# Eight landing places for the first conditioning panels, and the linear attention's decays made among the even features

## The reference, cut to what matters

```python
cond = jax.nn.silu(c)
mod = (cond @ w_ada[l] + b_ada[l]).reshape(B, N_SUB, 3, D_MODEL)
y = swiglu(modulate(x, mod, 0), ffn_w_in[l, 0], ffn_w_out[l, 0])
...
log_a = [(jax.nn.log_sigmoid(((h @ a1[d]) @ a2[d] + ab[d]).astype(jnp.float32)) / GLA_TAU)
         .reshape(bsz, t, GLA_HEADS, GLA_DK) for d in range(2)]
qk = jax.nn.silu(dwconv1d(jnp.concatenate([mq, mk], axis=-1), conv_w, conv_b))
```

## Time and profile before

| what | value |
|---|---|
| median of the runs | 3091.85 us |
| the profiled execution's own time | 3098.78 us |
| its span, first to last instruction | 3096.8 us |
| TensorE matmuls busy | 2802.9 us (91%) |
| VectorE | 1875.1 us (61%) |
| ScalarE | 1033.0 us (33%) |
| GpSimd | 197.4 us (6%) |
| mean granted clock of TensorE | 0.952 |
| moved by DMA | 469.59 MB, mean 152 GB/s |

### The profile page before, as it was taken

The page is one execution under the profiler, slowest core; times in us unless marked ns, Lnnn a source line. Parts: engine busy times, 40 slices in busy tenths (PEclk is TensorE's granted clock), DMA queues, the critical chain, the costliest instruction groups (busy, mean ns, idle before and its releaser), DMA issues.

```text
span 3096.8 us, 47653 instructions
## 1 busy us (share of the span) xinstructions
PE 2802.9 (91%) x18018; PEld 2359.1 (76%) x18018; DVE 1875.1 (61%) x3213; ACT 1033.0 (33%) x1331; POOL 197.4 (6%) x89
## 2 busy tenths in 40 slices
PE   2999999999999998999899556999999899979998
PEld 2998877899998887899778444587744767748887
DVE  5785354677775854667474466477732676662881
ACT  1432132443532124153443552333300644431211
POOL 0000000000000000000044000144300000000000
PEclk9999999999999998999999678999999999969999
DMA  7786633577574842456242100222234221103441
GB/s 260 275 315 253 230 108 123 204 272 285 206 270 163 321 141 96 163 177 234 93 178 95 63 1 34 82 95 90 103 158 160 83 81 55 68 14 123 150 174 70
DMA packets 109673, 469.59 MB, mean 152 GB/s; under 512 B 7020, under 2 KB 60856, under 8 KB 62136
## 3 DMA queue, kind: packets, MB, share of 16 engines
q1 hardware_dynamic: 109496, 467.19, 41.7%
HBM read 466.10 MB, written 1.06 MB: 151 GB/s over the span
## 4 chain that ended last, share of the span: by engine, by line
issue 53%; PE 31%; DVE 7%; DVEq 4%; ACT 2%; POOLq 1%; ACTq 1%
PE accs L786 9%; PE accs L674 4%; PE accs L687 2%; PE accs L689 2%; PE accs L688 2%; DVEq L2574 2%; PE accs L1134 2%; PE accs L1135 1%; PE accs L1136 1%; DVE arena L2551 1%; DVE normed L86 1%; POOLq L1339 1%; PE mix L1185 1%; ACT arena L76 1%; PE mix L833 1%
## 5 line engine op out<-in xcount | busy, mean ns | idle before, releaser
L687 PE MATMUL accs<-normed_r,arena_r 128*128 128x256 f32 (+2 forms) x1864 | 585.6, 314 | 20.4 <-DVE cond_panel_r L86 6.1
L688 PE MATMUL accs<-arena_r 128*128 128x256 f32 (+1 forms) x2090 | 594.8, 285 | 0.0
L689 PE MATMUL accs<-normed_r,panel_r 128*128 128x256 f32 (+2 forms) x1872 | 585.5, 313 | 0.0
L674 PE MATMUL accs<-normed,panel 128*128 128x256 f32 x2176 | 485.3, 384 | 6.3 <-ACTq L469 3.0
L674 PEld LDWEIGHTS accs<-normed,panel 128*128 128x128 f32 x2176 | 415.2, 192 | 71.1 <-ACTq L469 4.3
L86 DVE TENSOR_TENSOR panel_r<-panel,arena_r 128x1024 fp32r<-128x1024 f32 (+1 forms) x240 | 319.8, 1332 | 129.8 <-ACTq L1378 90.7
L688 PEld LDWEIGHTS accs<-arena_r 128*128 128x128 f32 x2090 | 395.4, 189 | 2.2 <-issue 0.2
L687 PEld LDWEIGHTS accs<-normed_r,arena_r 128*128 128x128 f32 (+1 forms) x1864 | 351.1, 188 | 56.4 <-issue 12.9
L1377 ACT ACTIVATE arena_r<-panel 128x1024 fp32r<-128x1024 f32 (+1 forms) x240 | 275.4, 1147 | 303.7 <-PE accs L689 115.3
L689 PEld LDWEIGHTS accs<-normed_r,panel_r 128*128 128x128 f32 (+1 forms) x1872 | 350.9, 187 | 23.9
L2551 DVE SCALAR_TENSOR_TENSOR arena<-accs,vectors,arena 128x189 f32<-128x189 f32 (+2 forms) x704 | 279.5, 428 | 94.6 <-issue 63.4
(11 more groups left out here) (375 smaller groups left out, 4175.5 us busy)
## 6 DMA issues: line engine op xcount, KB each, us to landing
panel<-w SPq DMA_DIRECT2D x250, 1024.0 KB, 4.9
panel<-w SPq DMA_DIRECT2D x48, 1408.0 KB, 7.9
cond_panel<-wc SPq DMA_DIRECT2D x56, 1024.0 KB, 6.9
normed<-wc SPq DMA_DIRECT2D x48, 1024.0 KB, 7.6
arena<-wc SPq DMA_DIRECT2D x16, 1024.0 KB, 6.0
residual<-xs SPq DMA_DIRECT2D x2, 1024.0 KB, 8.3
residual<-crows SPq DMA_DIRECT2D x2, 512.0 KB, 9.3
arena<-cond_row_kept SPq DMA_DIRECT2D x2, 512.0 KB, 6.7
```

Source lines behind the costliest of these rows:

```text
L674: mm = pe.matmul(acc[b][:, o:o + ntok], w[:, k * PANEL + j * P:k * PANEL + j * P + P], rhs(k), start=(k == 0), stop=(k == KD - 1))
L687: pe.matmul(out, hi[:, k, 0:m], src_hi(k), start=clear and k == 0, stop=False, skip_group_check=True)
L688: pe.matmul(out, hi[:, k, 0:m], src_lo(k), start=False, stop=False, skip_group_check=True)
L689: mm = pe.matmul(out, lo[:, k, 0:m], src_hi(k), start=False, stop=last and k == n - 1, skip_group_check=True)
```

## The change

Two things, which share no stage.

In the head every one of the eight conditioning panels gets a landing place of its own: the two of before, the first half of the residual tile, and five regions of the arena that hold nothing yet. SP issues all eight with no wait; the vectors come after panel 1, the latents after panel 4, weight panel 0 after panel 5, weight panel 1 after panel 7, then constants, tables and weight panels 2 and 3. No semaphore is new: panels 2 and 3 share one, 4 and 5 share one, and later waits on these are raised. VectorE weighs panels 0 and 1 before its arithmetic, 2 to 4 in the middle of it, 5 to 7 after it, and makes the low part of weight panel 0 after panel 6. The barrier of the head is gone. The first input is made two chunks at a time with a signal for each pair, and the low part of weight panel 1 between the third pair and the last. The bias matmul and its copy go behind weight panel 3 of `in00`.

In the even stage TensorE does the four decay matmuls after feature panel 0. ScalarE adds the bias into the unused ends of the four weight slots and takes the magnitude during panel 1, Exp before panel 2 and Ln before panel 3; VectorE combines them before the convolutions. Silu of the convolved channels goes from panels 12 and 13 to the beginnings of panels 10 and 11. After the barrier VectorE copies the combined decays into `logd` and clears `gsuff`, for one direction and then the other, and only then clears `gpairs` and masks the near product.

The diff, in the order of the program: tiles, semaphores, then SyncE, TensorE, ScalarE and VectorE.

```diff
+        head_slots = [H[:, :, 0:T], cond_slot1[:, :, :], X[:, :, 0:T]] + [region(2048 * i, KD, PANEL) for i in range(HEAD - 3)]
...
-        gabs = region(E_T + 2048, 2, 1024)
+        decay_kept = [t[:, KD * PANEL:KD * PANEL + 512] for t in slots]
+        decay_ln = [region(E_T + 8192, 2, 512), region(13312, 2, 512)]
...
+        head_landed = [(cond_landed[0], 16), (cond_landed[1], 16), (S("context_loaded"), 32), (S("context_loaded"), 32),
+                       (S("masks_loaded"), 32), (S("masks_loaded"), 32), (S("pair_loaded"), 16), (S("hankel"), 16)]
...
-            load_cond("head", 0, 0)
-            load_cond("head", 0, 1)
-            sp.dma_start(cols[:, :], io["cols"]).then_inc(S("cols_loaded"), 16)
+            for i in range(HEAD):
+                sp.dma_start(head_slots[i], wc[i:i + 1, :, :].rearrange("a p (k c) -> p (a k) c", k=KD)).then_inc(head_landed[i][0], 16)
+                if i == 1:
+                    sp.dma_start(cols[:, :], io["cols"]).then_inc(S("cols_loaded"), 16)
+                if i == 4:
+                    sp.dma_start(X[:, :, lat], xs[:, :, lat]).then_inc(S("latents_moved"), 16)
+                if i == 5:
+                    load_static(G["in00"], 0)
+            load_static(G["in00"], 1)
             sp.dma_start(cst[:, m1:NCST], io["consts"][:, m1:NCST]).then_inc(S("consts_loaded"), 16)
+            sp.dma_start(cst[:, 0:m0], io["consts"][:, 0:m0]).then_inc(S("loaded"), 16)
             sp.dma_start(poolw[:, :, :, :], io["poolw"]).then_inc(S("loaded"), 16)
             sp.dma_start(relb[:, :], io["rel_bias"]).then_inc(S("loaded"), 16)
+            load_static(G["in00"], 2)
+            load_static(G["in00"], 3)
             sp.wait_ge(S("consts_loaded"), 16)
             sp.dma_start(a2w[32:96, :], io["a2w"]).then_inc(S("loaded"), 16)
-            for i in range(2, HEAD):
-                load_cond("head", 0, i)
...
-            def gla():
+            def decays():
+
                 pe.wait_ge(S("rank_ready"), 1)
...
-                pe.wait_ge(S("decay_read"), 2)
...
-            pe.wait_ge(S("loaded"), 80)
-            pe.matmul(mix[0:4, 0, 0:384], relb[:, :], const("onehot")[0:32, :], start=True, stop=True).then_inc(S("bias_mm"), 1)
-            stage_end(pe, count)
...
                         split_up(G[name], it, u, 2 * l + f)
+                        if name == "in00" and isinstance(it, int) and (it, u) == (0, 3):
+                            pe.wait_ge(S("loaded"), 64)
+                            pe.matmul(mix[0:4, 0, 0:384], relb[:, :], const("onehot")[0:32, :], start=True, stop=True).then_inc(S("bias_mm"), 1)
...
                             kept_features(G["even"], 0, u, 0)
+                        if u == 0:
+                            decays()
+                    pe.wait_ge(S("decay_read"), 2)
...
-                for d in range(2):
-                    act.wait_ge(S("decay_mm"), d + 1)
...
+                            if step == 0:
+                                act.wait_ge(S("decay_mm"), d + 1)
+                                for c in range(2):
+                                    act.eng.activation(decay_kept[2 * d + c], mix[:, 2 * d + c, :], ACT.Identity, bias=col("gla_ab_2", 2 * d + c))
+                                act.drain().then_inc(S("decay_read"), 1)
+                            elif step == 1:
+                                for c in range(2):
+                                    act.activation(decay_ln[d][:, c, :], decay_kept[2 * d + c], ACT.Abs)
+                            elif step == 2:
+                                act.activation(decay_ln[d], decay_ln[d], ACT.Exp, scale=-1.0)
+                            else:
+                                act.activation(decay_ln[d], decay_ln[d], ACT.Ln, bias=one_col).then_inc(S("decay_ln"), 1)
+
                     for u in range(14):
+                        if u in (2, 3):
+                            decays(u)
+                        if u in (10, 11):
+                            c = 4 * (u - 10)
+                            act.wait_ge(S("ml_conv"), c + 4)
+                            act.activation(mqk[:, c:c + 4, :], mqk[:, c:c + 4, :], ACT.Silu)
...
+                            if u == 1:
+                                decays(r)
...
             def first_input():
-                for k in range(KD):
...
+                dve.wait_ge(S("latents_moved"), 16)
+                for c in range(0, KD, 2):
+                    for k in (c, c + 1):
+                        dve.eng.tensor_scalar(h_raw[:, k, :], X[:, k, lat], mods1[:, 0, 8 + k:9 + k], mods1[:, 0, k:k + 1], ALU.mult, ALU.add)
+                    dve.drain()
+                    dve.tensor_copy(h_hi[:, c:c + 2, :], h_raw[:, c:c + 2, :])
+                    dve.tensor_tensor(h_lo[:, c:c + 2, :], h_raw[:, c:c + 2, :], h_hi[:, c:c + 2, :], ALU.subtract)
+                    dve.drain().then_inc(S("h_ready"), 2)
+                    if c == 4:
+                        low(G["in00"], 0, 1)
...
             def gla():
-                dve.eng.memset(gsuff[:, :, :], 0.0)
+                for d in range(2):
+                    for c in range(2):
+                        dve.eng.tensor_copy(logd[:, d, 512 * c:512 * c + 512], decay_kept[2 * d + c])
+                    dve.eng.memset(gsuff[:, d, :], 0.0)
+                    dve.drain().then_inc(S("gla_sums"), 1)
                 dve.eng.memset(gpairs[:, :, :], 0.0)
...
+            dve.wait_ge(S("row_ready"), 1)
+            for i in range(2):
+                cond_weigh("head", i, i % 2)
             dve.wait_ge(S("cols_loaded"), 16)
...
             dve.drain().then_inc(S("lb_diff"), 1)
+            for i in range(2, 5):
+                cond_weigh("head", i, i % 2)
...
-            for i in range(HEAD):
+            for i in range(5, HEAD):
                 cond_weigh("head", i, i % 2)
+                if i == 6:
+                    low(G["in00"], 0, 0)
             cond_take("head")
-            stage_end(dve, count)
...
                     cond_take("even")
+                    for d in range(2):
+                        dve.wait_ge(S("decay_ln"), d + 1)
+                        for c in range(2):
+                            stt(decay_kept[2 * d + c], decay_kept[2 * d + c], 0.0, decay_ln[d][:, c, :], ALU.min, ALU.subtract)
```

66 lines of the change are left out of this document (21 added, 45 removed).

## The result

| | before | changed |
|---|---|---|
| median, same session, 5 runs each | 3093.37 us | 3073.37 us |
| lowest and highest | 3090.39, 3101.20 | 3072.48, 3078.38 |
| ratio, 95% interval | | 0.9932 [0.9919, 0.9945] |
| the profiled execution's own time | 3098.78 | 3072.94 |
| span | 3096.8 | 3071.1 |

What follows compares the result with a forecast made beforehand. TensorE, busy nearly all the span, was taken as the bound, so its standstills count. Head 12.5 gained, bias matmul 0.7 lost, decays 12.7 gained: 24.5 off 3098.8 gives 3074.3, against the median 3067.4 us; range 3061 to 3077.

Steps and rivals of the forecast that it cites:

- Arrivals in the head: Head: loads land 2.5 us apart, VectorE's weighing ends so that input making starts at 41.7 and TensorE at 43.9.
- The pause: Panel 0 of the first GEMM: TensorE pauses 3 us before the last input piece; a clock fall was counted at 1.0.
- (a): Even features: TensorE's eight decay records move between panels 0 and 1 and cost 1.9 us, or 3.8 if not clock-bound.
- (b): Even features: ScalarE's decay steps fit its idle waits, 5.9 us into 7.36 and Ln's 3.7 into the next; nothing uncovered.
- Rival 2: Even features: ScalarE's cover fails and 4 to 12.2 us come back, giving 3072 to 3080; chance 0.08.
- (c): Before the convolutions: VectorE's four combinations, 0.8 us each, 3.2 in all, are covered by a wait of 4.2.
- (d): End of the even features: moving Silu out of the tail into ScalarE's waits in panels 10 and 11 gains 3.1 us.
- Rival 1: Head: the queue delivers a panel every 3.1 us, so 3.0 us less gain, giving 3070; chance 0.08.
- Rival 3: First GEMM: TensorE's clock is held at 1.2 GHz behind the pause, 5.7 us more per panel, up to 3187; chance 0.03.
- Rival 4: Head or decays: one of the two parts brings nothing because something else is late behind it, 3079 to 3080; chance 0.05.
- theory A: Whole program, posed for the experiments: what a stage gains reaches the end whole.
- Theory B: Later stages, posed for the experiments: reaching them at another moment changes which short bursts run slow, by several microseconds.

Runs made afterwards that it cites:

- experiment 7: The changed kernel with only the bias matmul and its copy moved ahead of weight panel 0: 3073.04 us.
- experiment 8: The kernel before with the head's part and, of the even stage's edits, only Silu ahead of panels 10 and 11: 3084.17 us.
- experiments 1 and 2: Each part alone against the kernel before: the head's part 3084.72 us, ratio 0.9977; the decays' part 3080.98 us, ratio 0.9955.
- experiment 1: The changed kernel with every decay edit undone, so the head's part alone: 3084.72 us, ratio 0.9977 to the kernel before.
- experiments 3: The changed kernel with two more clearing passes on VectorE ahead of the first input: 3075.14 us.
- experiment 11: The combined version with three clearings on VectorE ahead of the first input: 3067.02 us.
- the combined version: Changed kernel plus early bias matmul, separate semaphores for panels 4 and 5, bounds' arithmetic before panel 2, both low parts later: 3062.48, then 3063.95 us.

## Why the prediction was right, and where it wasn't

The sign and the size were right, 3073.4 in a range of 3061 to 3077, for the two reasons given. The forecast of 3067.4 itself was 6.0 too low: 1.5 because the kernel before now had a median of 3093.37 and not 3091.85, 4.5 because 20.0 us came off and not 24.5. By its own steps:

- **Arrivals in the head: mis-sized.** The forecast had the first weighing at 8.9, the third at 18.2, the fifth at 25.8 and the first input at 41.7. The profile has 9.73, 19.30, 27.17 and 43.34: 1.6 late, and the first working matmul at 45.58 is outside the 43 to 45 that it named as a sign. Half of it (0.8) is the first landing: the first weighing varied from 7.7 to 9.8 between executions; I had one sample, and took it for the value. Another 0.5 is the rate: three loads between 19.30 and 27.17 took 2.6 us each instead of 2.5. The last 0.3 is VectorE's own work, 16.2 us from the fifth weighing to the first input instead of 15.9. The slower bound (3.1 us a load) and the 2.93 of the rule that the prediction cited from the Trainium skill were both farther off. Another page of the Trainium skill, Perfetto Trace Analysis, Roofline, says that with only one core of a pair active the bound is the 16 DMA engines at about 435 GB/s, and names 358 as the share when both are; three 1.05 MB loads in 7.87 us are 400 GB/s, and the trace agrees with that page, not with the rule as I cited it.
- **The pause: placed right, and its cost left open rightly.** 2.41 us instead of 3; I put 1.0 on a fall of the clock that either comes (2.0) or doesn't (0). In the first profile it did not, in the second of the same kernel it did, for 1.3. So 1.6 lost on the arrivals and 1.0 not spent on the clock nearly cancel, which is luck: 11.9 gained at panel 1 instead of 12.5.
- **Bias matmul: forecast 0.7.** 0.9 at its place, next to nothing net (experiment 7). That it had been hidden in the idle head was no gain to lose.
- **(a) records of the decays: 1.9 forecast, 2.0 measured**; the shift goes from -14.0 to -11.9 across them.
- **(b) ScalarE's cover held**, with 1.07, 0.95 and 3.26 us of wait left. The near miss was panel 1: 2.74, 1.28 and 2.19 are 6.2 us, where I had put 5.9 into 7.36. Rival 2 is out by its own rows.
- **(c) VectorE's combinations** took 4.88 us for four, not 3.2, but not because each was priced too low: three took 0.69, below the 0.8 of the forecast, and the first 2.58. Timelines of VectorE and GpSimd in the changed kernel:

```profile
1622.00 2.58 DVE L91 SCALAR_TENSOR_TENSOR panel<-panel,arena 128x512 f32<-128x512 f32 x1 [0.40 <-issue]
...
1624.66 0.69 DVE L91 SCALAR_TENSOR_TENSOR panel<-panel,arena 128x512 f32<-128x512 f32 x1
```

```profile
1621.63 2.40 POOL L1351 TENSOR_TENSOR panel_r<-panel,arena_r 128x1024 fp32r<-128x1024 f32 x1 [2.81 <-ACTq L1398]
```

  GpSimd's subtraction of a low part ran from 1621.63 to 1624.03, and the first combination ended at 1624.58. The first convolution behind, 1.56 us where the next took 0.75, also overlaps such a subtraction and ended 0.55 behind it. That GpSimd held VectorE up is what the times suggest; no run tests it. The convolution still waited 1.68 us, so it cost nothing.
- **(d) Silu: 3.1 forecast; the barrier 3.2 nearer** (-12.2 to -15.4) and 3.0 by experiment 8.
- **Barrier to loop: 7.0 forecast, 6.9 measured.** Sum of the decays at the loop's start: 13.0 (-14.0 to -27.0), 13.1 in the run with them alone; forecast 12.7.
- **Rival 1** did not decide (2.6 us a load). The sentence "That the eight transfers are not really out at once can't be" is contradicted by SyncE's rows in the last section. **Rival 3**: the first GEMM ran its other panels as before, 120.2 us at a clock of 1.00 as in the earlier trace rows:

```profile
56.30:176.50 120.20, 118.10 (x987) 116.23 (x986) 90.86 (x110) 51.44 (x54) 0.00 (x0) 1.00 0.76 267
```

- **Rival 4** is out by experiments 1 and 2.
- **The step that failed** is the last of the sum: "set against the median it gives 3067.4". The stages' gains, 11.9 and 13.0, make 24.9, or 24.0 with the bias matmul's 0.9; between the two profiled executions I found 25.8, between the medians 20.0. The execution that was profiled before was 5.4 us above the median of its session, the one after 0.4 below. Such a surplus sits, as far as the runs show, in the low level of short bursts (3.8 us at the spread and just behind it), and the longer executions of a kernel have, as a rule, the lower mean clock (experiment 1). A part of it changes when the kernel changes, a part from one execution to the next. So a stage's gain is sound, and its sum over the program is uncertain by some 5 us for a reason that no stage's row shows. I had no term for that; the range covered it by luck of the other bounds.

What stays open is what decides the level of a burst. As a rule for every execution, theory A is refuted by experiments 3, 8 and 11. Theory B holds only in a weak form: the combined version won 3.9 us between 1220 and 1310 in both profiles and the changed kernel nothing in both, and with the delay of experiment 11 all runs had a higher mean clock. The third, the execution itself, has its part too: the same instructions spread at 2.05 us in three executions and at 3.68 in one. How the 5 us divide between these two isn't shown. The Trainium skill, TensorE: Matmul & The Clock Gate, What's actually happening, says that the hardware's look at TensorE's activity runs freely and doesn't start with the kernel, so that the number of slow matmuls varies from run to run. The traces agree that the number varies: the same kernel's clock fell after its pause in one execution and not in the other, and experiment 8's spread came out otherwise than the changed kernel's. What makes it vary no run here shows.

## What to carry to other kernels

A gain read from one stage's rows can be right to half a microsecond and still reach the end some 5 us changed, because TensorE's granted clock in later short bursts (here 16 matmuls at 2.05 or 3.78 us) changes with the kernel and from one execution to the next; compare shifts at milestones of two traces, ask whether a step lies where the change does, and profile a kernel more than once before calling a step its own. When all loads of a head are issued at once, fill each wait for a landing with whatever doesn't need it, give no two loads one semaphore, and let nothing come ahead of the last piece that the bound engine waits for: all of it together put panel 1 another 7.5 us forward and took 10 us off the median. When several instructions are merged into one row, look at them singly before dividing (2.58 and three of 0.69 are not four of 1.2). A row that stands for one landing is one sample; here it varied by 2 us.

## What was not expected

SyncE stalled while issuing. Its timeline in the changed kernel:

```profile
4.45 5.39 SPq L574 DMA_DIRECT2D arena<-wc  x1
9.88 0.97 SPq L574 DMA_DIRECT2D arena<-wc  x1
...
11.37 3.10 SPq L574 DMA_DIRECT2D arena<-wc  x1
14.51 4.44 SPq L534 DMA_DIRECT2D panel<-w  x1
```

An issue takes 0.65 us in the earlier trace rows. Here that of the fourth conditioning panel, behind three panels and the vectors, took 5.39 us and ended at 9.84, when the first had landed (its weighing began at 9.73); those of the sixth and of weight panel 0 took 3.10 and 4.44. So the eight were not really out at once, as the prediction had it; it looks as if the fourth and some behind it entered only as others landed. I see no cost in it, since the loads landed at 2.6 us each all the same, but what stands behind them in SyncE's order comes that much later. And a delay of 6.5 us in the head made the combined version only 3.1 us slower (experiment 11).
